# Rank-one expert sums every 12 steps instead of every 14, and their row gathers issued later, in two halves

## The reference, cut to what matters

```python
experts = jnp.take_along_axis(cidx, top_p, axis=-1)
gate = jax.nn.softmax(top_s, axis=-1)
act = jax.nn.gelu(jnp.einsum('nd,nhkd->nhk', h, u[experts]).astype(jnp.float32), approximate=False)
return jnp.einsum('nhk,nhkd->nd', (gate * act).astype(h.dtype), v[experts])
```

## Time and profile before

| what | value |
|---|---|
| median of 3 runs | 4392.64 us (4392.03 to 4392.75) |
| the profiled execution | 4392.64 us, span 4390.8 us |
| value stage | about 3225 to 4350 us of the span |
| PE busy, whole span | 4263.5 us (97%) |
| DVE busy, whole span | 2958.3 us (67%) |
| PEclk | the granted TensorE clock, mean 0.989 of full speed |

### The profile page before, as it was taken

One profiled execution on the slowest core, in us unless ns is written; L12 is line 12 of the kernel. 1 busy time (PEld: TensorE's weight loads), 2 busy tenths in 40 slices (PEclk: granted clock), 3 DMA queues, 4 the chain that ended last, 5 costly groups with the idle time before them and its releaser, 6 DMA issues.

```text
span 4390.8 us, 67457 instructions
## 1 busy us (share of the span) xinstructions
PE 4263.5 (97%) x28423; PEld 4021.6 (92%) x28423; DVE 2958.3 (67%) x4430; ACT 1214.4 (28%) x1614; POOL 717.5 (16%) x744
## 2 busy tenths in 40 slices
PE   7999999999999989999999999999999999999997
PEld 7999889998899979988899999999999999999997
DVE  4241463332334356699998988998878888888887
ACT  3221352332212121223232222222232222222233
POOL 1010002332000000000011111111022333333310
PEclk9999999999999989999999999999999999999998
DMA  6433226776343543355599999999999999999983
GB/s 195 112 102 103 86 64 201 235 237 204 107 135 111 154 105 73 71 123 124 150 284 284 284 280 279 279 291 275 274 336 348 355 348 355 343 367 343 356 325 123
DMA packets 599373, 968.32 MB, mean 221 GB/s; under 512 B 143889, under 2 KB 406033, under 8 KB 565016
## 3 DMA queue, kind: packets, MB, share of 16 engines
q1 hardware_dynamic: 508560, 519.33, 41.6%
q0 software_dynamic: 84992, 434.18, 27.0%
q10 hardware_dynamic: 5520, 10.49, 0.8%
HBM read 873.63 MB, written 85.75 MB: 218 GB/s over the span
## 4 chain that ended last, share of the span: by engine, by line
PE 87%; DVE 9%; issue 2%; ACT 1%; DMA 1%; ACTq 0%; DVEq 0%; SPq 0%
PE pair L1932 29%; PE pair L2351 24%; PE pair L2273 22%; PE quad L1932 2%; PE pair L2308 2%; DVE w_lo L1619 2%; PE quad L2333 1%; PE quad L1896 1%; PE pair L1896 1%; DVE turned L1614 1%; PE quad L2103 1%; ACT w_hi L873 1%; PE quad L2146 1%; DVE ts L1635 1%; PE pair L1968 1%
## 5 line engine op out<-in xcount | busy, mean ns | idle before, releaser
L2273 PE MATMUL pair<-act_hi,w_hi 128*128 128x448 f32 x2048 | 758.8, 371 | 15.2 <-DVE w_lo L1619 15.2
L2273 PE MATMUL pair<-act_lo,w_hi 128*128 128x448 f32 x2048 | 749.4, 366 | 0.0
L2273 PE MATMUL pair<-act_hi,w_lo 128*128 128x448 f32 x2048 | 749.1, 366 | 0.0
L1932 PE MATMUL pair<-act_hi,w_hi 128*128 128x288 f32 x3264 | 719.0, 302 | 29.4 <-DVE act_lo L1324 12.5
L1264 DVE TENSOR_TENSOR w_lo<-w_raw,w_hi 128x2048 fp32r<-128x2048 f32 x103 | 236.2, 2293 | 747.1 <-ACT w_hi L873 747.1
L1932 PE MATMUL pair<-act_hi,w_lo 128*128 128x288 f32 x3264 | 702.4, 297 | 0.0
L1932 PE MATMUL pair<-act_lo,w_hi 128*128 128x288 f32 x3264 | 701.4, 297 | 0.0
L2351 PE MATMUL pair<-wx_hi,v_hi 128*128 128x384 f32 x2016 | 677.9, 336 | 4.1 <-DVE wx_lo L1786 3.3
L2351 PE MATMUL pair<-wx_hi,v_lo 128*128 128x384 f32 x2016 | 674.3, 334 | 0.0
L2351 PE MATMUL pair<-wx_lo,v_hi 128*128 128x384 f32 x2016 | 674.1, 334 | 0.0
L1932 PEld LDWEIGHTS pair<-act_hi,w_hi 128*128 128x128 f32 x3264 | 526.1, 190 | 67.7 <-issue 61.5
(11 more groups left out here) (328 smaller groups left out, 5525.2 us busy)
## 6 DMA issues: line engine op xcount, KB each, us to landing
w_raw<-in_peer_u_dram SPq DMA_DIRECT2D x512, 256.0 KB, 5.8
v_raw<-in_peer_v_dram SPq DMA_DIRECT2D x256, 512.0 KB, 7.7
w_raw<-in_w_in_dram SPq DMA_DIRECT2D x64, 1024.0 KB, 7.2
gelu_dram<-tmp SPq DMA_DIRECT2D x128, 224.0 KB, 7.9
gmat_dram<-gmat SPq DMA_DIRECT2D x48, 512.0 KB, 11.5
a_back<-gelu_dram SPq DMA_DIRECT2D x128, 192.0 KB, 5.9
g_back<-gmat_dram SPq DMA_DIRECT2D x64, 384.0 KB, 6.7
w_raw<-in_w_out_dram SPq DMA_DIRECT2D x16, 1024.0 KB, 8.2
```

Of the source, the lines that this page charges most:

```text
L1932: op = m_(pair[out][:, hf, 0:TH], w[:, k, :], x[:, k, hf * TH:(hf + 1) * TH], start=(starts and k == ks[0] and i == 0), stop=(ends and k = ...
L2273: op = m_(pair[0][:, n % 2, 0:TU], w[n % 2][:, k, :], x[:, k, 0:TU], start=(k == 0 and i == 0), stop=(k == KD - 1 and i == 2))
```

## The change

Three edits. `SP_STEP` takes 12 steps between expert sums instead of 14: (2,4), (3,0), (3,12), (4,8), (5,4), (6,0), ... (25,8). `ROWS_AT` places k = 0 at the first slot behind the step of the expert sum before, instead of the last slot ahead of it. And the entries do other things: rows 0 and 1 at k = 0, rows 2 and 3 at k = 1, cells or weights at k = 2. So for a step x = `SP_STEP[q - 1]` with d = 0, 4, 8 or 12, the slots of k = 0, 1, 2 are those that VectorE does 3, 7 and 11 steps behind x, and `expert_sums(q)` stands 12 steps behind x; where one of the four extra slots at d = 6 falls in between, k = 1 or k = 2 comes earlier.

```diff
-SP_STEP = [divmod(2 * KD + 4 + 14 * q, KD) for q in range(2 * SP_N)]
+SP_STEP = [divmod(2 * KD + 4 + 12 * q, KD) for q in range(2 * SP_N)]
...
-ROWS_AT = {max(i for i, x in enumerate(SUMS) if x < SP_STEP[q]) + S_RING + k: (q + 1, k) for q in range(2 * SP_N - 1) for k in range(3)}
+ROWS_AT = {min(i for i, x in enumerate(SUMS) if x > SP_STEP[q]) + S_RING + k: (q + 1, k) for q in range(2 * SP_N - 1) for k in range(3)}
...
                     q, k = ROWS_AT[i]
                     if k == 0:
                         pool.wait_ge(e_mm, q)
-                        for j in range(COLS):
-                            gather_row(q, j)
-                    elif k == 1 and q % 2 and 2 <= q // 2 + 1 < SP_N:
+                    if k < 2:
+                        gather_row(q, 2 * k)
+                        gather_row(q, 2 * k + 1)
+                    elif q % 2 and 2 <= q // 2 + 1 < SP_N:
                         gather_cells(q // 2 + 1)
-                    elif k == 1 and q % 2 == 0 and q >= 4:
+                    elif q % 2 == 0 and q >= 4:
                         weigh(q // 2)
```

## The result

The changed kernel takes 4673.45 us (4672.02 to 4677.75, 4 runs) against 4392.69 us: ratio 1.0639, interval 1.0621 to 1.0658. That is 281 us or 6.4% slower. The forecast was 190.5 us slower, 4583 us, with 4630 us as its high end: the sign and the mechanism in the main came as forecast, the size did not.

A forecast was written before the change was run, and what follows sets the result against it. The prediction took TensorE, busy all the time in the expert-sum stage, as the bound. Stands of 62.4 + 73.6 + 6.5 = 142.5 us plus 48 us of slow clock gave 190.5 us on 4392.64, so 4583 us, range 4505 to 4630.

The forecast's parts named there:

- What bounds the kernel: In the expert-sum stage TensorE is busy all the time, so everything that makes it wait is added in full.
- What the change can give: Over the whole kernel, a gain of 0 to 1 us, taken as 0; denser row traffic priced at nothing.
- The weights: At 13 even-q expert sums, weights made at k = 2 come 4.8 us late each, 62.4 us in all.
- The rows: At 16 expert sums, rows 2 and 3 land late, a 4.6 us stand each, 73.6 us; hidden at 13 even q.
- the term L: Time from issue of the slot's gather at k = 1 to landing of the second row behind it: 9.7 us.
- q = 5 and q = 14: Expert sums where k = 1 comes earlier: stands of 3 us (0 to 4) and 3.5 us, together 6.5 us.
- The clock: Behind 30 of 31 stands TensorE's clock falls, 1.6 us lost each, 48 us; bounds 0 and 53.
- Worse: At the expert sums, rows take 11.6 us every time because gathers pile up: 248 us, 4640 us; chance 0.1.
- the clock stays up: Behind the stands TensorE's clock does not fall, so only 142.5 us of stands count: 4535 us; chance 0.1.
- rows land in time: At the expert sums only the weights are late: 4476 us if rows come wholly free, otherwise 4530 us; chance 0.15.
- no difference: At the expert sums weights are met sooner and rows land in 5 us: 4393 us; chance 0.03.
- faster: GpSimd no longer blocks on PE and slots come sooner: 7 us gained at most, 4386 us; chance 0.02.

The follow-up runs named there:

- Stride alone: The kernel before with one edit, an expert sum every 12 steps instead of 14, rows still issued early and together: ratio 0.9993 (0.9984 to 1.0003).
- the run with the rows together: The changed kernel with all four rows issued at k = 0, none at k = 1, cells and weights still at k = 2: 4578.73 us.
- halving its loads of `v`: The changed kernel with half of each of SP's loads of `v` from the 17th on, leaving out half of the dense result: 4628.34 us.
- one row less: The changed kernel without row 1, so only row 0 is gathered at k = 0 and one token's result is left out: 4649.71 us.
- both cuts: The changed kernel without row 1 and with half of each of SP's loads of `v` from the 17th on, on another chip: 4614.71 us.
- the repeated run: The changed kernel itself measured once more, beside the kernels with less traffic: 4678.73 us.
- the fill of 60 matmuls: The changed kernel with 60 extra matmuls of 128 columns, no part of the computation, ahead of each of the 31 later expert sums: 4646.01 us.
- 14 steps and the late order: The changed kernel with 14 steps between expert sums again, its late and split row issue kept: 4475.29 us.

## Why the prediction was right or wrong, by its steps

- **What bounds the kernel.** Right. With PE 100% busy in the stage, each stand went into the time in full: of the 287.6 us, 220.9 are waits and 61 slow matmuls behind them (below).
- **What the change can give.** Right, nothing. Stride alone is at 0.9993, and the closer packing by itself costs nothing.
- **The weights.** The mechanism and the 13 places were right, as the run with the rows together shows, 4.4 us each instead of 4.8. But the rows end later still, so in the changed kernel they are hidden: its list of waits has only rows. "Alternate stands end with the weights and with the rows" was wrong.
- **The rows.** This is the step that failed, the term L. The form of the sum (L + 3.3 - 8.4) holds: in the round shown L is 3343.47 - 3332.07 = 11.4 us, and L - 5.1 = 6.3 is the idle time of PE in its timeline, 6.34. Over 31 places the mean stand of 7.1 us makes L 12.2, not 9.7. That is 220.9 - 142.5 = 78 of the 97 us that the forecast was short of the profiled run. The prediction had named this sign of being wrong: stands far from 4.7 us on average. Three choices made L too small. I took it from the time in which the queue moved 2.12 MB in the earlier trace rows, not from a landing, so that whatever passes between the two is missing: by the packets in the trace of the changed kernel 0.5 us from the end of a row's last packet to the release of TensorE. I took 0.7 us off because the other queue would fall quiet, when in fact halving its loads of `v` still gave 1.3 us for each stand: it was not quiet. And I took the queue as empty at k = 1, when the pair of k = 0, 8.3 us ahead of it, was partly still on its way (0.7 us for each stand from one row less). The other queue from 3332 to 3343, during the transfer of the round shown, had 37.2% where the earlier trace rows had 28.3%:

```profile
q1 hardware_dynamic: 662, 1.61, 37.2%
```

  By the packets L is 1.7 us to the slot's first, 9.2 of transfer and 0.6 to the release at even q (but 14), 11.5 in all. At odd q (but 5) it is 3.5, 8.9 and 0.5, 12.9 in all. The prediction had 1.6 and 8.8 and took off 0.7. The upper bound of 6.5 us for a stand came from the longest landing of a lone slot, but two rows more stood behind the slot; a bound from a single transfer is none for three in a row. With both cuts made, 24 us of waits over the forecast stay; L is then 10.4 us at odd and 10.7 at even q, of it 0.4 and 0.6 behind the last packet.
- **q = 5 and q = 14.** q = 14 stood for 4.71 us instead of 3.5, which is L again. q = 5 stood for 7.69 us instead of 3 (6.04 in the repeated run), outside the 0 to 4 us that I allowed: its two batches, 5 us apart, queued up behind each other, and with one row less the stand was 2.53.
- **The clock.** The mechanism was right and is shown by the fill of 60 matmuls. The size was not, and this is the second term that failed: 287.6 - 220.9 = 66.7 us are left behind the waits where I had 48, and the clock of the stretch is 0.89 where I had 0.94. Windows with the expert sums alone, changed kernel and before (busy PE is the figure behind the comma):

```profile
3300.00:4398.00 1098.00, 110.66 (x496) 21.16 (x496) 0.89 0.73 268
3300.00:4240.00 940.00, 59.64 (x496) 12.94 (x496) 1.00 0.94 352
```

  The expert sums take 51 us more in all; 1.79 us each where the clock stays low to their end, less where it recovers sooner. The dense matmuls between two of them take 0.33 us longer than in the kernel with the stride alone, 10 us in all. Together that is 61 us, 2.0 for each stand where I had 1.6. The other 5 lie elsewhere, 2.3 of them ahead of the first expert sum. I had measured the low stretch behind one gap; why these stretches cost more is open.
- **The rivals.** "Worse" was the nearest: stands of 6.5 us from rows that pile up, 4640 us, chance 0.1. It had the kind of cause right, rows that take 11.6 us because gathers pile up, and was still 33 us short. That the clock stays up, that rows land in time, no difference and faster are all out.

## What to carry to other kernels

Where the engine that bounds a kernel waits in program order, ask of each gather how much of that engine's work lies between its issue and its use, and compare this with the landing of the last of the batch, slot and earlier batches on its queue included: here 8.4 us were left for a chain of 15.5. The room that an early issue seems to waste is what hides it: moved by 8.4 us, it cost 281. A stand of the matmul engine is then paid for twice, once as the wait and, where the clock falls, once more, about 2 us here, in slow work behind it.

## What was not expected of the hardware

With 14 steps and the late order, stands of 0.9 to 4.3 us came in one trace, and the clock did not fall behind all of them. Windows at a stand of 2.95 us (the first two) and one of 3.78 us (the last two); the third figure from the end is the granted clock:

```profile
3320.00:3324.00 4.00, 1.05 (x11) 0.35 (x13) 1.91 (x3) 2.71 (x4) 0.08 (x1) 1.00 1.04 424
3324.00:3328.00 4.00, 4.00 (x29) 3.16 (x22) 0.62 (x2) 0.00 (x0) 0.00 (x0) 1.00 0.97 372
3453.00:3457.00 4.00, 0.22 (x5) 0.09 (x8) 1.89 (x3) 2.70 (x4) 3.05 (x4) 1.00 1.02 413
3457.00:3461.00 4.00, 4.00 (x20) 1.79 (x21) 0.00 (x0) 0.00 (x0) 0.95 (x1) 0.61 1.04 378
```

Behind the first, 29 matmuls in 4 us at the full 2.4 GHz; behind the second, 20 at a mean clock of 0.61, most of it at 1.2 GHz. That is nine matmuls less in 4 us, at 0.1745 us each 1.6 us. But the length of a stand does not decide it alone. In the same trace, q = 13 and q = 31:

```profile
3725.97 1.92 PE L2334 MATMUL quad<-e_rows,e_w 128*32 128x512 f32 x16 [3.32 <-DMA e_rows<-in_peer_v_dram,e_row]
4318.20 3.52 PE L2334 MATMUL quad<-e_rows,e_w 128*32 128x512 f32 x16 [2.08 <-DMA e_rows<-in_peer_v_dram,e_row]
```

Behind 3.32 us the expert sum ran at full speed, behind 2.08 us at the low clock. What else decides is not shown here; stands of about 3 us brought the fall in some places and not in others, and all 31 of the changed kernel, of 4.7 us and more, brought it.

And 512 KB gathered by rows took longer to land than 1 MB gathered by a slot. For the rows the medians were 9.6 us (the last of the four) and 8.0 us (the first, in the repeated run). For the slots of the same two traces they were:

```profile
DMA to landing us min/median/max: 5.4/6.2/12.5
DMA to landing us min/median/max: 5.4/5.8/11.1
```

The rows' landing is set by what stands ahead and beside, more than by their own bytes.
